# Moving the S5 parameter arithmetic from VectorE to GpSimd, with its transfers first

## The reference, cut to what matters

```python
dt = jnp.exp(log_dt)[:, None]
mag = jnp.exp(a_re * dt)
ab_re = mag * jnp.cos(a_im * dt)
ab_im = mag * jnp.sin(a_im * dt)
den = a_re * a_re + a_im * a_im
nr, ni = ab_re - 1.0, ab_im
cf_re = ((nr * a_re + ni * a_im) / den)[..., None]
cf_im = ((ni * a_re - nr * a_im) / den)[..., None]
bb_re = cf_re * b_re - cf_im * b_im
bb_im = cf_re * b_im + cf_im * b_re
```

## Time and profile before

| | |
|---|---|
| median of 3 runs | 2051.36 us |
| profiled execution | 2051.92 us, its span 2050.1 us |
| busy share of the span | PE 92%, PE weight loads 89%, DVE 49%, POOL 38%, ACT 35% |
| chain that ended last, by engine | PE 72%, DVE 13%, DMA 4%, POOL 4%, SP's queue 3% |
| 0 to 52.56 us | PE busy 35.62 us, DVE 39.38 us |
| 52.56 to 202.64 us | PE busy 123.85 us, DVE 130.35 us |

### The profile page before, as it was taken

The page is one execution under the profiler, slowest core; times in us unless marked ns, Lnnn a source line. Parts: engine busy times, 40 slices in busy tenths (PEclk is TensorE's granted clock), DMA queues, the critical chain, the costliest instruction groups (busy, mean ns, idle before and its releaser), DMA issues.

```text
span 2050.1 us, 34797 instructions
## 1 busy us (share of the span) xinstructions
PE 1895.8 (92%) x14967; PEld 1823.0 (89%) x14967; DVE 1008.4 (49%) x1512; ACT 712.3 (35%) x1225; POOL 784.1 (38%) x475
## 2 busy tenths in 40 slices
PE   6987999899998999879998989999999899899996
PEld 5987898899988998879997989988998799899996
DVE  7987123732328983267653212174333588524223
ACT  3354223434542222233333541244445222223221
POOL 2643456333223333332331784553232222334440
PEclk8888899999999999999998999999999999999998
DMA  8343334322245544525442332432222655443321
GB/s 148 115 148 114 89 93 95 98 73 69 58 121 153 171 145 115 130 68 150 134 146 87 90 87 69 98 104 68 72 63 72 168 168 173 105 136 93 93 88 57
DMA packets 349776, 221.58 MB, mean 108 GB/s; under 512 B 49588, under 2 KB 338536, under 8 KB 347064
## 3 DMA queue, kind: packets, MB, share of 16 engines
q1 hardware_dynamic: 347320, 189.75, 35.0%
q10 hardware_dynamic: 2304, 29.62, 3.9%
HBM read 171.65 MB, written 38.50 MB: 103 GB/s over the span
## 4 chain that ended last, share of the span: by engine, by line
PE 72%; DVE 13%; DMA 4%; POOL 4%; SPq 3%; ACT 2%; issue 2%; ACTq 0%; DVEq 0%; POOLq 0%
PE ring L710 53%; PE ring L693 3%; DMA sb_w_raw<-in_w_in 2%; PE aux L854 2%; PE aux L931 2%; POOL sb_w_lo L603 2%; DVE sb_s_mat_prod L1380 2%; PE aux L1020 1%; PE aux L866 1%; PE aux L1007 1%; SPq L517 1%; PE aux L760 1%; DVE sb_s_gelu_lo L1380 1%; PE aux L976 1%; SPq L557 1%
## 5 line engine op out<-in xcount | busy, mean ns | idle before, releaser
L603 POOL TENSOR_TENSOR sb_w_lo<-sb_w_raw,sb_w_hi 128x1024 fp32r<-128x1024 f32 x246 | 607.9, 2473 | 1168.4 <-ACT sb_w_hi L1079 1166.9
L1079 ACT ACTIVATE sb_w_hi<-sb_w_raw 128x1024 fp32r<-128x1024 f32 x246 | 259.6, 1056 | 596.7 <-DMA sb_w_raw<-in_w_in 379.5
L710 PE MATMUL ring<-sb_u_hi,sb_w_hi 128*128 128x264 f32 x2624 | 372.9, 297 | 27.9 <-DVE sb_tmp_dve L1448 25.4
L710 PEld LDWEIGHTS ring<-sb_u_hi,sb_w_hi 128*128 128x128 f32 x2624 | 346.5, 198 | 39.4 <-DVE sb_tmp_dve L1448 26.4
L710 PE MATMUL ring<-sb_u_lo,sb_w_hi 128*128 128x264 f32 x2624 | 347.4, 286 | 0.0
L710 PE MATMUL ring<-sb_u_hi,sb_w_lo 128*128 128x264 f32 x2624 | 343.5, 284 | 0.0
L710 PEld LDWEIGHTS ring<-sb_u_lo,sb_w_hi 128*128 128x128 f32 x2624 | 332.1, 190 | 0.0
L710 PEld LDWEIGHTS ring<-sb_u_hi,sb_w_lo 128*128 128x128 f32 x2624 | 327.8, 188 | 0.0
L1109 ACT ACTIVATE sb_tmp_act<-ring 128x528 f32<-128x528 f32 x112 | 68.1, 608 | 105.7 <-PE ring L710 92.6
L1311 ACT ACTIVATE sb_att_scores<-sb_att_scores,sb_att_neg_max 128x208 f32<-128x208 f32 x128 | 58.5, 458 | 91.4 <-DVE sb_att_neg_max L1639 91.4
L710 PE MATMUL ring<-sb_y_hi,sb_w_hi 128*128 128x264 f32 x672 | 89.1, 285 | 0.0
(11 more groups left out here) (301 smaller groups left out, 2915.9 us busy)
## 6 DMA issues: line engine op xcount, KB each, us to landing
sb_w_raw<-in_w_in SPq DMA_DIRECT2D x166, 512.0 KB, 4.1
sb_s_loaded<-s_matrices ACTq DMA_DIRECT2D x16, 1808.0 KB, 7.9
s_matrices<-sb_s_phase SPq DMA_DIRECT2D x16, 528.0 KB, 3.2
s_matrices<-sb_s_mbt SPq DMA_DIRECT2D x16, 512.0 KB, 2.8
s_matrices<-sb_s_ca SPq DMA_DIRECT2D x16, 512.0 KB, 4.3
sb_w_raw<-in_w_gla_out SPq DMA_DIRECT2D x16, 512.0 KB, 3.8
sb_w_raw<-in_w_attn_out SPq DMA_DIRECT2D x16, 512.0 KB, 3.6
sb_w_raw<-in_s_w_glu SPq DMA_DIRECT2D x16, 512.0 KB, 3.6
```

Source lines behind the costliest of these rows:

```text
L603: pool.tensor_tensor(WL[:, w], WR[:, w], WH[:, w].bitcast(F32), ALU.subtract).then_inc(lo_ready, 1)
L710: last = pe.matmul(RING[:, 2 * r + hf, 0:HALF], w[:, n % SLOTS, kt, :], xx[:, kt, HALF * hf:HALF * hf + HALF], start=(term == 0 and kt == ...
L1079: act.activation(WH[:, w], WR[:, w], ACT.Copy).then_inc(hi_ready, 1)
```

## The change

s5_prepare now runs on POOL, on the same tiles. POOL has no fused scalar_tensor_tensor here, so stt does a tensor_scalar into a thirteenth slot of SP_ and a tensor_tensor. The exponent's integer is made by one tensor_scalar with an int32 output. The denominator of the input factor stays on DVE, early (den_ready). lo_part(0) to lo_part(3) stand between the parts: lo_part(0) behind the third, lo_part(3) behind the last. SP issues the five S5 row transfers ahead of the tokens, and "s5p" is the first entry of AUX, so PE turns those rows first. input_matrix waits on phase_in.

```diff
-AUX = ([(-1, ("xin", i)) for i in range(9)] + [(-1, ("prm", 0)), (-1, ("bias", 0)), (-1, ("s5p", 0))]
+AUX = ([(-1, ("s5p", 0))] + [(-1, ("xin", i)) for i in range(9)] + [(-1, ("prm", 0)), (-1, ("bias", 0))]
...
         def _(sp):
-            sp.dma_start(MIN[:], meta_tokens).then_inc(x_loaded[4], 16)
-            for t in range(4):
-                sp.dma_start(XIN[:, t], x[0, P * t:P * t + P, :]).then_inc(x_loaded[t], 16)
...
             sp.dma_start(LDR[:], s5_log_dt.rearrange("l (q g) -> (l q) g", g=2)).then_inc(s5_rows, 16)
+            sp.dma_start(MIN[:], meta_tokens).then_inc(x_loaded[4], 16)
+            for t in range(4):
+                sp.dma_start(XIN[:, t], x[0, P * t:P * t + P, :]).then_inc(x_loaded[t], 16)
...
+            def stt(o, a, x, b, op0, op1):
+                link(pool.tensor_scalar(SP_[:, 12], a, x, None, op0))
+                return pool.tensor_tensor(o, SP_[:, 12], b, op1)
...
+            def exponential(o, x, k, r, q):
...
+                for f in (720, 120, 24, 6, 2, 1):
+                    link(stt(q, q, 1.0 / f, r, ALU.add, ALU.mult))
+                link(pool.tensor_scalar(IK[:], k, 127.0, 8388608.0, ALU.add, ALU.mult))
+                link(stt(o, q, 1.0, IK[:].bitcast(F32), ALU.add, ALU.mult))
...
+                den, nr, cfr, cfi = sp(13), sp(14), CF[:, 0], CF[:, 1]
+                pool.wait_ge(den_ready, 1)
...
             for ly in range(DEPTH):
                 work = phases(ly)
+                if ly == 0:
+                    aux_read(pool, -1, ("s5p", 0))
+                    for i, _ in enumerate(s5_prepare()):
+                        if i >= 2:
+                            lo_part(i - 2)
                 for b in range(NB):
-                    lo_part(ly * NB + b)
+                    if ly or b >= 4:
+                        lo_part(ly * NB + b)
...
+            dve.wait_ge(s5_rows, 16 * (2 * DEPTH + 1))
+            dve.tensor_copy(LDB[:], LDR[:].unsqueeze(2).broadcast_to([DEPTH * PAIRS, 2, S5_STATE])
+                            ).then_inc(dt_wide, 1)
...
+            link(tt(den, den, im2, ALU.add))
+            dve.reciprocal(den, den).then_inc(den_ready, 1)
...
                 if ly == 0:
-                    for _ in prepare:
-                        pass
                     input_matrix(0)
                     s5_matrices(0, 0)
...
             def input_matrix(m):
 
                 dve.wait_ge(s5_par, 32 * m + 32)
+                dve.wait_ge(phase_in, 1)
...
-            prepare = s5_prepare()
-            aux_read(dve, -1, ("s5p", 0))
-            next(prepare)
-            next(prepare)
```

More of the change, by code:

```diff
@@ L223, in trunk @@
         r = [o_mix + 4096, o_mix + 8192]
-        SP_ = sb("s5_small", [P, 12, DEPTH, PAIRS], at=r)
+        SP_ = sb("s5_small", [P, 13, DEPTH, PAIRS], at=r)
         IK = sb("s5_int", [P, DEPTH, PAIRS], I32, at=r)
@@ new lines, in double_angle, with complex_mult @@
+            def double_angle(s, c, t):
+                link(tt(t, s, s, ALU.mult))
+                link(stt(s, s, 2.0, c, ALU.mult, ALU.mult))
+                link(pool.tensor_scalar(c, t, -2.0, 1.0, ALU.mult, ALU.add))
+            def complex_mult(ore, oim, are, aim, bre, bim, t1, t2):
+                tt(t1, are, bre, ALU.mult)
+                link(tt(t2, aim, bim, ALU.mult))
+                link(tt(ore, t1, t2, ALU.subtract))
+                tt(t1, are, bim, ALU.mult)
+                link(tt(t2, aim, bre, ALU.mult))
+                link(tt(oim, t1, t2, ALU.add))
@@ new lines, in s5_prepare, with pw @@
+            def s5_prepare():
+                are, aim, ldt = (S5P[:, :, i] for i in range(3))
+                dt, mag, phi, k, r, q, s, c, t1, t2 = (sp(i) for i in range(3, 13))
+                exponential(dt, ldt, k, r, q)
+                link(tt(t1, are, dt, ALU.mult))
+                yield
+                exponential(mag, t1, k, r, q)
+                link(tt(phi, aim, dt, ALU.mult))
+                link(pool.tensor_scalar(k, phi, 1.0 / (2 * math.pi), 12582912.0, ALU.mult, ALU.add))
+                link(pool.tensor_scalar(k, k, 12582912.0, None, ALU.subtract))
+                c1 = 6.28125
+                c2 = float(np.float32(2 * math.pi - c1).view(np.uint32) & np.uint32(0xFFFFF000))
+                c2 = float(np.uint32(int(np.float32(2 * math.pi - c1).view(np.uint32)) & 0xFFFFF000)
+                           .view(np.float32))
+                c3 = 2 * math.pi - c1 - c2
+                link(stt(r, k, -c1, phi, ALU.mult, ALU.add))
+                link(stt(r, k, -c2, r, ALU.mult, ALU.add))
+                link(stt(r, k, -c3, r, ALU.mult, ALU.add))
+                link(pool.tensor_scalar(r, r, 0.25, None, ALU.mult))
+                yield
+                link(tt(t2, r, r, ALU.mult))
+                link(pool.tensor_scalar(s, t2, 1.0 / 362880, None, ALU.mult))
+                for f in (-5040.0, 120.0, -6.0):
+                    link(stt(s, s, 1.0 / f, t2, ALU.add, ALU.mult))
+                link(stt(s, s, 1.0, r, ALU.add, ALU.mult))
+                link(pool.tensor_scalar(c, t2, -1.0 / 3628800, None, ALU.mult))
+                for f in (40320.0, -720.0, 24.0, -2.0):
+                    link(stt(c, c, 1.0 / f, t2, ALU.add, ALU.mult))
+                link(pool.tensor_scalar(c, c, 1.0, None, ALU.add))
+                yield
+                double_angle(s, c, t1)
+                double_angle(s, c, t1)
+                def pw(ri, n):
+                    return APW[:, ri, :, :, n]
+                pool.memset(pw(0, 0), 1.0)
+                pool.memset(pw(1, 0), 0.0)
+                tt(pw(0, 1), mag, c, ALU.mult)
+                link(tt(pw(1, 1), mag, s, ALU.mult))
+                for n, (a, b) in ((2, (1, 1)), (3, (2, 1)), (4, (2, 2))):
+                    complex_mult(pw(0, n), pw(1, n), pw(0, a), pw(1, a), pw(0, b), pw(1, b), t1, t2)
+                yield
+                den, nr, cfr, cfi = sp(13), sp(14), CF[:, 0], CF[:, 1]
+                pool.wait_ge(den_ready, 1)
+                link(pool.tensor_scalar(nr, pw(0, 1), 1.0, None, ALU.subtract))
+                tt(t1, nr, are, ALU.mult)
+                link(tt(t2, pw(1, 1), aim, ALU.mult))
+                link(tt(cfr, t1, t2, ALU.add))
+                link(tt(cfr, cfr, den, ALU.mult))
+                tt(t1, pw(1, 1), are, ALU.mult)
+                link(tt(t2, nr, aim, ALU.mult))
+                link(tt(cfi, t1, t2, ALU.subtract))
+                link(tt(cfi, cfi, den, ALU.mult))
+                yield
+                double_angle(s, c, t1)
+                double_angle(s, c, t1)
+                tt(t1, s, s, ALU.mult)
+                link(tt(t2, c, c, ALU.mult))
+                link(tt(t1, t1, t2, ALU.add))
+                link(pool.tensor_scalar(t1, t1, -0.5, 1.5, ALU.mult, ALU.add))
+                tt(AB[:, 0], c, t1, ALU.mult)
+                tt(AB[:, 1], s, t1, ALU.mult)
+                link(tt(t2, mag, mag, ALU.mult))
+                tt(AB[:, 2], t2, t2, ALU.mult).then_inc(phase_in, 1)
+                yield
```

126 lines of the change are left out of this document (26 added, 100 removed).

## The result

The changed kernel took 2054.45 us (median of 20 runs), the kernel before 2046.96 (median of 20 on the same chips). The ratio is 1.0033, 95% interval 1.0019 to 1.0047: 6.8 us slower, by the ratio. Single runs spread over 14 to 16 us (2040.43 to 2056.90 before, 2048.70 to 2062.27 after). The forecast was 2053.0 us, +1.6 on the kernel before, with "within 0.2%" as the likeliest class (0.53). The time is near the forecast and within the range. The size of the loss is not: 0.33% is its class "slower" (0.38), and the loss is four times the forecast one. Part of the agreement in the time is luck. The forecast was added to 2051.36 us, a median of 3 runs, and over 20 runs the same kernel's median is 4.4 us lower. The profiled execution after took 2060.71 us, its span 2058.9.

What follows compares the result with a forecast made beforehand. DVE's queue was taken to bound the stretch from 52.56 to 202.64 us; PE's delay of 6.0 less 4.4 won gave +1.6 us, 2053.5 profiled, 2053.0 after taking off 0.56; range 2047.5 to 2062.

Steps and rivals of the forecast that it cites:

- within 0.2%: Whole kernel: time not to be told from no change, 2047.3 to 2055.5 us; chance 0.53.
- slower: Whole kernel: time above the 2047.3 to 2055.5 us that can't be told from no change; chance 0.38.
- What the most is that can be won: Before the first decay step: without parameter work it begins 4.44 us earlier, no more, since ACT's logarithm is next.
- d: Time by which PE's row of blocks (ga, gk, gv) starts later, forecast 6.0 us; the end moves by d - 4.44.
- three signs of being wrong: POOL tensor_scalar outside 0.24 to 0.33 us, DVE's u operations keeping 0.7 beside POOL, PE waiting for DVE before step matrices.
- tensor_scalar was taken at 0.28: POOL's parameter arithmetic: one tensor_scalar takes 0.28 us, 0.36 linked; 45 of them among 77 instructions ahead of lo_part(0).
- rival (a): POOL ahead of lo_part(0): tensor_scalar at 0.40 us makes d 15, the end +10.7, 2062 us; chance 0.36.
- POOL against DVE: Beside DVE's u operations: each small POOL operation costs DVE 0.2 us, a turn takes 0.87; the last 6 of 77 alternate.
- The transfers: Start of the kernel: five S5 transfers put token transfers back 2.7 us, and u by 0.6, to 34.5 us.
- block a u operation for 2.4 us: DVE's u operations: lo_part(0) gets its turn among them, ends at 42.4 us at the latest, and blocks DVE that long.
- the start of the norm sum: Behind the first transfers and residual copies: the norm sum starts at 18.0 to 18.8 us instead of 18.23.
- a stretch in which DVE sets the time: From 52.56 to 202.64 us: DVE is late for most further step matrices; the only place where the change can act.

Runs made afterwards that it cites:

- e3: Kernel before with all S5 parameter arithmetic replaced by three memsets to a constant; ratio 0.9967 to the kernel before.
- e2: Changed kernel with lo_part(0) and (1) behind the first parameter part, lo_part(2) and (3) later, and C turned behind gk1, not gk3; ratio 1.0012.
- g4: Changed kernel with POOL's one-operation tensor_scalars written with two operations, and C turned behind gk1 instead of gk3; ratio 1.0008 to the kernel before.
- g1: Kernel before with POOL's lo_part(0) also waiting until DVE has made the last low part of u; ratio 1.0051.
- f1: Changed kernel with POOL's one-operation tensor_scalars written with two operations, the added one changing nothing; ratio 0.9981 to the kernel before.
- g3: Changed kernel with low parts placed where their operands are ready and POOL's one-operation tensor_scalars written with two operations; ratio 0.9997 to the kernel before.
- g2: Kernel before with lo_part(0) waiting for the last low part of u, and C turned behind gk1 instead of gk3; ratio 1.0053.

## Why the prediction was right and wrong

**The limit (the step "What the most is that can be won") failed.** It named ACT's logarithm as what comes next behind DVE's queue, 4.44 us later, and took d - 4.44. Before the first decay step DVE also makes the first step's products, and these need C, which PE turns behind gk3: a wait on PE's row that the kernel before hides by 0.7 us. C came 8.8 us late (87.23 for 78.39), 0.7 was covered, and DVE's first product moved by 8.2, the first step matrices by 8.4. e3 shows the wait with DVE idle, e2 and g4 show it going away when C is turned early, and g4 shows the logarithm as the limit behind it, with d - 4.44 right to 0.3 us. g1 adds that the old order had little slack either, by way of the gates: of 7.4 us at gk0 6.1 arrived at the first step matrices. The prediction named three signs of being wrong, and all three came: a tensor_scalar outside 0.24 to 0.33, u operations that keep their 0.7 beside POOL, and PE waiting for DVE again.

**d was 6.0 and came out at 8.8** (gk0 at 61.38 for 52.56). At the end of the first block, where the sum took it, it was 10.3 (56.10 for 45.81), and the gate matmuls gave 1.5 back, which the sum had not in it. Three terms of the sum were mis-sized. (1) tensor_scalar was taken at 0.28; it is 0.37 with one operation and 0.24 with a multiply and an add, and 38 of the 45 ahead of lo_part(0) have one. This is the condition of rival (a), "from about 0.32 a piece, where d passes 8.5", and f1 shows that it decides between this loss and none. (2) POOL against DVE: forecast 0.2 lost by DVE for each POOL operation and 0.87 for a turn. DVE lost 0.03, a turn was 0.71, but 17 of the 77 stood beside u, not 6, at 0.71 in place of the 0.42 of the 60 before them (7.54 to 32.81). (3) The transfers were to put u back by 0.6 us, to 34.5; it began at 32.81.

**Wrong in a way that helped.** lo_part(0) was to block a u operation for 2.4 us; it came behind u and blocked none. And the steps gave 2.9 us back, which the prediction had not in it; 1.9 of these are less busy time of PE for the same 605 matmuls. Of +8.4 at the first step matrices +5.3 were left at 345 us, by chance near the 4.4 that d = 8.8 gives in the prediction's own formula. A time within the range shows nothing on the mechanism here.

**Right:** the start of the norm sum behind the transfers (18.36, in 18.0 to 18.8), POOL's start, the first block bound by lo_part(0), the residual copies undisturbed, low parts 1 to 3 in time for PE, the parameters ready before they are needed (at 72.20 for 72.5; the in-factor products ended by 80.71). One reading was off without a consequence: the low part that PE's first block needed was there at 17.3 before, not at 19.6, since the row of 4.66 us holds two of them.

**What the steps give or take** is worth as much as the change: from the first to the last step matrices the kernel before takes 102.6 us, the changed one 99.8, f1 94.0, g3 101.2. In part it is the alignment of two queues. DVE's timeline at the copies (sb_s_brep) of the fifth step matrices, before:

```profile
147.22 2.96 DVE L1814 COPY sb_s_brep<-sb_s_mb 128x512 f32<-128x512 f32 x2
```

and f1:

```profile
144.40 0.76 DVE L1837 COPY sb_s_brep<-sb_s_mb 128x512 f32<-128x512 f32 x2
```

Before, POOL had begun a low part at 147.48, for 2.41 us; in f1 it began at 146.09, behind the copy. This shows the collision, but not the gain: the fifth step matrices came at 150.28 before and at 150.44 in f1, where PE wasn't waiting for the copy. The lead comes behind them. The windows from the fifth to the sixth and from the sixth to the seventh step matrices (columns as in rows 1), before:

```profile
150.28:165.01 14.73, 9.83 (x82) 9.62 (x83) 14.38 (x24) 9.42 (x15) 10.03 (x13) 0.96 0.65 188
165.01:178.96 13.95, 13.95 (x82) 13.95 (x83) 10.03 (x20) 5.20 (x10) 3.26 (x2) 0.67 0.28 94
```

and f1:

```profile
150.44:162.00 11.56, 9.78 (x85) 9.56 (x83) 11.17 (x21) 6.68 (x12) 7.14 (x10) 1.00 0.58 172
162.00:173.09 11.09, 9.82 (x83) 9.66 (x84) 10.78 (x21) 8.04 (x13) 3.91 (x5) 1.00 0.47 149
```

The first window is bound by DVE: PE does the same work, and f1 is 3.2 us shorter because PE waits less. In the second PE is busy all the time before, at a granted clock of 0.67, and DVE isn't the limit; f1 does the same matmuls at 1.00 in 9.82 us. Over all the steps f1's 8.6 us are 4.7 us less busy time of PE (75.42 for 80.13, with 572 and 573 matmuls) and 3.9 us less waiting. So PE's speed is at least as large a part as its waiting. And the prediction's picture of a stretch in which DVE sets the time holds for four of the seven windows only: in the other three PE was idle for less than 0.4 us before. Before, PE had been idle for 4.9 us of the window ahead of the slow one, in f1 for 1.8; that the one leads to the other isn't shown. Nor does an experiment show what makes the difference between f1, g3 and g4.

**Open:** what moves the kernels against each other by up to 8 us behind the first 345 us, where their instructions are the same. From the mark at 345 to the one at 2029 us, the kernel before, g2 and g4:

```profile
345.19:2029.29 1684.10, 1595.44 (x12929) 1542.47 (x12927) 803.61 (x1127) 588.78 (x1040) 626.40 (x331) 0.97 0.38 107
348.27:2040.40 1692.13, 1602.30 (x12929) 1548.85 (x12927) 801.94 (x1127) 588.07 (x1040) 625.38 (x331) 0.96 0.38 106
343.36:2021.70 1678.34, 1590.24 (x12929) 1539.44 (x12927) 801.76 (x1127) 588.82 (x1040) 626.01 (x331) 0.97 0.38 107
```

The same 12929 matmuls kept PE busy for 6.9 us more in g2, which took 8.0 us longer, and for 5.2 us less in g4, which took 5.8 us less. So most of the drift between these is TensorE's speed on equal work, as in the 16 gate matmuls (6.08 us before, 4.62 after). Whether that belongs to the kernel or to the one execution that was profiled, no run tells; runs of one kernel spread as widely. So of the versions tried f1 is the best candidate, with 0.9981 (0.9961 to 1.0001); that it beats the kernel before isn't proven.
